# Later low halves, split sums of squares and a regrouped mixer projection in a two-block transformer kernel

## What is computed

```
def first_block(x, ...):                                  # DEPTH is 1
    x = x + 0.5 * rms_norm(swiglu(rms_norm(x, ffn1_pre_g[l]), ffn1_w_gu[l], ffn1_w_down[l]), ffn1_post_g[l])
    y = hybrid_mixer(rms_norm(x, mix_pre_g[l]), ...)      # RG-LRU and attention, then y @ w_o
    x = x + rms_norm(y, mix_post_g[l])
    x = x + 0.5 * rms_norm(swiglu(rms_norm(x, ffn2_pre_g[l]), ffn2_w_gu[l], ffn2_w_down[l]), ffn2_post_g[l])

def second_block(x, c, ctx, ...):                         # i = 0 a retention, i = 1 a neighbourhood attention
    for i in range(DEPTH_2):
        y_lat = mixer(modulate(h_lat, m_lat[0], m_lat[1]), ...)
        h_lat = layer_norm(DEEPNORM_ALPHA * h_lat + m_lat[2] * y_lat, ln_g[i, 0], ln_b[i, 0])
        f_lat = swiglu_2(modulate(h_lat, m_lat[3], m_lat[4]), ffn_w13[i], ffn_w2[i])
        h_lat = layer_norm(DEEPNORM_ALPHA * h_lat + m_lat[5] * f_lat, ln_g[i, 1], ln_b[i, 1])
        # in layer 0 the context h_ctx goes the same way

def swiglu(x, w_gu, w_down):
    gate, up = jnp.split(x @ w_gu, 2, axis=-1)
    return (jax.nn.silu(gate) * up) @ w_down
```

## Time and profile before

| | us |
|---|---|
| median of 3 runs (lowest and highest) | 3059.47 (3057.58 and 3062.56) |
| the profiled execution | 3062.67 |
| its span, first to last instruction | 3060.9 |
| PE busy | 2918.7 |
| DVE busy | 1477.6 |
| ACT busy | 1044.0 |
| POOL busy | 535.0 |
| mean granted TensorE clock, as a share of full speed | 0.977 |

### The profile page before, as it was taken

The page is one execution under the profiler, slowest core; times in us unless marked ns, Lnnn a source line. Parts: engine busy times, 40 slices in busy tenths (PEclk is TensorE's granted clock), DMA queues, the critical chain, the costliest instruction groups (busy, mean ns, idle before and its releaser), DMA issues.

```text
span 3060.9 us, 40191 instructions
## 1 busy us (share of the span) xinstructions
PE 2918.7 (95%) x16176; PEld 2480.4 (81%) x16176; DVE 1477.6 (48%) x2596; ACT 1044.0 (34%) x1813; POOL 535.0 (17%) x287
## 2 busy tenths in 40 slices
PE   7999989899998999999998899999998998999998
PEld 7888886888878868778685888888887777898887
DVE  5676569457674324242333735434564525642224
ACT  4322247442333422222222622122235535452222
POOL 1342200023231101111010011111102212012220
PEclk9999989899999999999999999999998999999999
DMA  3544312125443101111010023323312111122221
GB/s 137 177 158 169 107 64 74 65 90 173 149 160 123 58 28 62 49 48 63 28 62 21 29 90 119 102 74 109 128 49 89 56 57 66 63 76 105 102 95 37
DMA packets 84697, 268.81 MB, mean 88 GB/s; under 512 B 8992, under 2 KB 16544, under 8 KB 84128
## 3 DMA queue, kind: packets, MB, share of 16 engines
q1 hardware_dynamic: 84512, 266.25, 25.2%
HBM read 262.54 MB, written 2.10 MB: 86 GB/s over the span
## 4 chain that ended last, share of the span: by engine, by line
PE 61%; DVE 4%; ACT 2%; issue 1%; POOL 0%; DMA 0%; DVEq 0%; ACTq 0%; POOLq 0%; SPq 0%
PE ps L1348 18%; PE ps L1349 18%; PE ps L1350 18%; PE ps L1530 3%; PE ps L1580 1%; PE ps L1521 1%; PE ps L1564 1%; PE ps L1553 1%; ACT t_whi L1610 1%; DVE t_misc L1916 0%; ACT t_h L1659 0%; DVE t_x L1938 0%; DVE t_wlo L1896 0%; DVE t_tmp L2248 0%; DVE t_misc L2256 0%
## 5 line engine op out<-in xcount | busy, mean ns | idle before, releaser
L1348 PE MATMUL ps<-t_h,t_whi 128*128 128x512 f32 (+1 forms) x2368 | 830.2, 351 | 28.0 <-POOL t_wlo L2330 19.9
L1349 PE MATMUL ps<-t_h,t_wlo 128*128 128x512 f32 (+1 forms) x2368 | 825.5, 349 | 0.0
L1350 PE MATMUL ps<-t_h,t_whi 128*128 128x512 f32 (+1 forms) x2368 | 824.3, 348 | 0.0
L2330 POOL TENSOR_TENSOR t_wlo<-t_raw,t_whi 128x1024 fp32r<-128x1024 f32 (+3 forms) x147 | 356.6, 2426 | 1542.4 <-ACT t_whi L1610 1542.3
L1348 PEld LDWEIGHTS ps<-t_h,t_whi 128*128 128x128 f32 x2368 | 455.2, 192 | 90.5 <-issue 18.9
L1349 PEld LDWEIGHTS ps<-t_h,t_wlo 128*128 128x128 f32 x2368 | 455.5, 192 | 54.8
L1350 PEld LDWEIGHTS ps<-t_h,t_whi 128*128 128x128 f32 x2368 | 454.5, 192 | 55.4
L1348 PE MATMUL ps<-t_hid,t_whi 128*128 128x256 f32 (+1 forms) x1306 | 426.9, 327 | 11.2 <-DVE t_hid L2028 4.0
L1896 DVE TENSOR_TENSOR t_wlo<-t_raw,t_whi 128x1024 fp32r<-128x1024 f32 (+3 forms) x180 | 222.5, 1236 | 440.1 <-ACT t_whi L1610 439.9
L1610 ACT CAST t_whi<-t_raw 128x1024 fp32r<-128x1024 f32 (+3 forms) x327 | 326.3, 999 | 310.2 <-PE ps L1350 279.2
L1349 PE MATMUL ps<-t_hid,t_wlo 128*128 128x256 f32 (+1 forms) x1306 | 423.0, 324 | 0.0
(11 more groups left out here) (249 smaller groups left out, 3813.8 us busy)
## 6 DMA issues: line engine op xcount, KB each, us to landing
t_raw<-in_gu SPq DMA_DIRECT2D x176, 512.0 KB, 3.2
t_raw<-in_ada SPq DMA_DIRECT2D x96, 512.0 KB, 3.2
t_raw<-in_dn SPq DMA_DIRECT2D x52, 512.0 KB, 3.5
t_raw<-in_dn SPq DMA_DIRECT2D x24, 384.0 KB, 3.2
t_raw<-in_ret_v SPq DMA_DIRECT2D x16, 512.0 KB, 3.2
t_raw<-in_ret_qk SPq DMA_DIRECT2D x16, 512.0 KB, 3.2
t_raw<-in_ret_g SPq DMA_DIRECT2D x16, 512.0 KB, 3.1
t_raw<-in_ret_o SPq DMA_DIRECT2D x16, 512.0 KB, 3.5
```

The costliest lines, as they stand in the source:

```text
L1348: e.matmul(out, whi, xlo, start=first, stop=False, skip_group_check=shared)
L1349: e.matmul(out, wlo, xhi, start=False, stop=False, skip_group_check=shared)
L1350: return e.matmul(out, whi, xhi, start=False, stop=last, skip_group_check=shared)
L2330: e.tensor_tensor(m.block(1, it.slot, n), m.raw(it), m.block(0, it.slot, n), ALU.subtract).then_inc(*S["lo_pool"].of(j))
```

## The change

The number of products is the same; the order of items, the engine of some low halves and the grouping of one projection change.

- **Low halves.** `give` puts a block's `prep_lo` into a list `lows`. While a chain runs or blocks are held, one block stays in it, so a low half stands one block later than its high half; `ready(j)` writes it out ahead of the first product that needs it. The choice between VectorE and GpSimd keeps its rule, but falls otherwise in places, since two kinds of chain last longer.
- **Squares and sums.** The item `sum` was two instructions, one for ScalarE and one for VectorE, at one place. Now `square` is ScalarE's item, and `sum` stands one chunk later where chunks arrive one by one (`late`).
- **Root.** For s = 1 of a norm over squares the chain starts after 4.5 instead of 1.6 units, which puts `root_sum` and `root_row` two steps of TensorE later in nf1, nm and nf2 (and in mixp and f2p one or two steps later).
- **Late work.** The chains of `alpha` and `ln_out` start after 14.0 instead of 0.5 units. The last attention stage ends them before it moves x.
- **by_steps.** All drains of the four step groups stand ahead of the `over` calls, and so ahead of the next blocks' high and low halves.
- **Mixer.** `probs(0)` stands two steps earlier; one `release` stands earlier; the output projection starts with six blocks of the first 256 tokens and two of the next 256 in step groups, where it was seven and one, and the blocks that were held are prepared ahead of the drains.

```diff
@@ -157,6 +158,8 @@
         keys = [(which, i + k) for k in range(w)]
+        while any(k in it["keys"] for it in adds for k in keys):
+            put("sum", **adds.pop(0))
         return (0 if which == "a" else 1024) + i * 256, [e for k in keys for e in slots.get(k, [])], keys
...
@@ -197,24 +200,32 @@
         where[j] = slot
-        if chains or state["held"] is not None:
+        busy = chains or state["held"] is not None
+        if busy:
             low[j] = "lo_dve"
...
         put("prep", j=j, slot=slot, after=after, lo=low[j])
-        if state["held"] is None:
-            put("prep_lo", j=j)
-        else:
-            state["held"].append((None, j))
+        lows.append(j)
+        split(1 if busy else 0)
...
+    def split(keep=0):
...
+        while len(lows) > keep:
+            put("prep_lo", j=lows.pop(0))
...
+    def ready(j):
...
+        while j in lows:
+            split(len(lows) - 1)
+        return j
...
-        held = state["held"]
-        for i in [i for i, (slot, _) in enumerate(held) if slot is None][::-1]:
-            put("prep_lo", j=held.pop(i)[1])
-        if held:
-            give(*held.pop(0))
+        split()
+        if state["held"]:
+            give(*state["held"].pop(0))
...
@@ -277,12 +290,14 @@
                 yield
-            for g, j, post in zip(groups, held, posts):
-                if si == len(segs) - 1:
+            for g, post in zip(groups, posts):
+                post(g)
+            if si == len(segs) - 1:
+                for g, j in zip(groups, held):
                     over(j, "ps", g.id)
-                post(g)
             for (_, _, nk, src, outs), j in zip(specs[4:], held[4:]):
                 (_, emptier, post), = outs
+                ready(j)
                 b = following()
...
@@ -331,17 +346,25 @@
-    def sum_add(inst, s, c, tile, ready, square, after=()):
-        it = put("sum", inst=inst, s=s, c=c, tile=tile, ready=ready, square=square, after=list(after), off=0)
-        if square and c >= 2:
-            it["off"], it["after"], keys = tmp("a", 256)
-            free(keys, ("acc", (inst, s, c)))
+    def sum_add(inst, s, c, tile, ready, square, after=(), late=False):
+        it = dict(inst=inst, s=s, c=c, tile=tile, ready=ready, square=square, after=list(after), off=0, keys=[])
+        if square:
+            if c >= 2:
+                it["off"], it["after"], it["keys"] = tmp("a", 256)
+                free(it["keys"], ("acc", (inst, s, c)))
+            put("square", **it)
+            if c >= 2:
+                adds.append(it)
+                while len(adds) > (1 if late and c < DC - 1 else 0):
+                    put("sum", **adds.pop(0))
+        else:
+            put("sum", **it)
...
         first = 0 if square else 2
-        sum_add(inst, s, j, tile, ready, square, state["acc_free"] if first <= j < first + 2 else ())
+        sum_add(inst, s, j, tile, ready, square, state["acc_free"] if first <= j < first + 2 else (), True)
         if j == DC - 1:
-            chains[s] = [1.6, chain(s)]
+            chains[s] = [4.5 if square and s == 1 else 1.6, chain(s)]
...
@@ -381,7 +404,7 @@
         if c == DC - 1:
-            chains[s + 10] = [0.5, later("alpha", s=s)]
+            chains[s + 10] = [14.0, later("alpha", s=s)]
...
@@ -418,7 +441,7 @@
         if out:
-            chains[s + 10] = [0.5, later("ln_out", inst=inst, ln=ln, s=s)]
+            chains[s + 10] = [14.0, later("ln_out", inst=inst, ln=ln, s=s)]
...
@@ -630,14 +653,13 @@
                          seats=[0, 1, 2, 3, 4, 5, 7, 4, 6, 5])
-        between = {1: lambda: v_turn(0, 6), 4: lambda: scores(0), 7: lambda: scores(1)}
+        between = {1: lambda: v_turn(0, 6), 4: lambda: scores(0), 7: lambda: scores(1), 9: lambda: probs(0)}
         state["held"] = []
...
                 release()
-        probs(0)
         v_turn(1, 4)
...
@@ -698,12 +720,12 @@
         each("rec_e", (1,))
+        release()
         cols.append(root_sums("ya", 1, 1, heads, False))
...
         apply("ya", 0, 0, heads)
-        release()
         each("rec_g", (0, 1, 2))
...
@@ -727,8 +749,9 @@
         groups = []
-        for i, (j, t0) in enumerate([(j, 0) for j in range(7)] + [(0, 256)]):
+        for i, (j, t0) in enumerate([(j, 0) for j in range(6)] + [(0, 256), (1, 256)]):
             b = 4 + i // 2
+            ready(held[j])
             if i % 2 == 0:
...
@@ -741,44 +764,42 @@
-        o_step(4, groups[:7], 0)
-        o_step(5, groups[:7], 0)
+        o_step(4, groups[:6], 0)
+        o_step(5, groups[:6], 0)
         cols = [root_sums("yl", s, 2 + s, lru) for s in range(2)]
...
         apply("ya", 1, 1, heads)
-        o_step(6, groups[:7], 0)
+        o_step(6, groups[:6], 0)
         put("root_row", inst="yl", s=0, off=offs[0], bank=2)
         apply("yl", 0, 2, lru)
-        o_step(7, groups[:7], 0)
+        o_step(7, groups[:6], 0)
         put("root_row", inst="yl", s=1, off=offs[1], bank=3)
...
         for k in heads:
-            o_step(k, groups[7:], 256)
+            o_step(k, groups[6:], 256)
         for k in lru:
-            o_step(k, groups[:7], 0)
-            o_step(k, groups[7:], 256)
+            o_step(k, groups[:6], 0)
+            o_step(k, groups[6:], 256)
+        while state["held"]:
+            release()
         state["held"] = None
+        for g in groups[6:]:
+            over(g.w, "ps", groups[7].id)
         for g in groups:
             o_post(g.j)(g)
-        over(held[0], "ps", groups[7].id)
-        late = block(("w_o", 7), (SLOT,))
...
-        def o_rest(j, w, t0):
+        held.append(block(("w_o", 7), (SLOT,)))
+        for j, t0 in [(6, 0), (7, 0)] + [(j, 256) for j in range(2, 8)]:
             b = bank()
-            g = put("mm", w=w, slot=where[w], lo=low[w], base=0, nk=DC, src=("y",), t0=t0, n=256, bank=b, po=0,
+            ready(held[j])
+            g = put("mm", w=held[j], slot=where[held[j]], lo=low[held[j]], base=0, nk=DC, src=("y",), t0=t0, n=256, bank=b, po=0,
                     before=seat(b, "drain_act", len(items)))
...
             if t0:
-                over(w, "ps", g.id)
+                over(held[j], "ps", g.id)
             o_post(j)(g)
-            return ("ps", g.id)
...
-        o_rest(7, late, 0)
-        for j in range(1, 8):
-            last = o_rest(j, (held + [late])[j], 256)
-        state["hid_free"] = [last]
+        state["hid_free"] = [("ps", g.id)]
         state["misc_free"] = [("y_lo", (3, 1))]
...
@@ -926,6 +948,8 @@
             state["acc_free"] = [("drain_dve", ("na_s", 1, 15, hd)) for hd in range(2)] + [("bm", (1, 3, 2, 1)), ("d_misc", "mask2")]
+            for s in (10, 11, 12):
+                force(s)
             put("move_x")
```

12 lines of the change are left out of this document (7 added, 5 removed).

## The result

The changed kernel is slower. Its median is 3069.43 us (3065.61 to 3075.18, seven runs) against 3059.47 us (3055.47 to 3063.34, seven runs) of the kernel before: a ratio of 1.0035, interval 1.0021 to 1.0048. I had forecast 3037.7 us with 3022 to 3052 as the range. The sign is wrong, and the measured median lies 32 us above the forecast.

A forecast was written before the change was run, and what follows sets the result against it. TensorE, busy 95% of the span, was taken to bound the kernel, leaving its gaps and slow stretches to win. Gains of 28.3 us less losses of 6.5 gave net 21.8, from 3059.47 to 3037.7 us, range 3022 to 3052.

The forecast's parts named there:

- End of the first FFN: Stall of 8.52 us near 396 us: later root and lagging low halves leave two short waits; gain 8 us, bounds 3.5 and 12.5.
- the two new waits that I forecast: End of first FFN, 394 to 401 us: 1.2 us for block 71's low half, 1.4 us for mixp's `root_sum`.
- rival (b): Waits are passed on: a later `root_sum` only moves the wait to the diagonal or next sum; 11 us less, 3049 us; chance 0.22.
- the mixer's probabilities: At 453 us TensorE's wait of 2.04 us, with its clock, is covered by two earlier steps; gain 3.7 us.
- What gets worse: Four step groups in by_steps: drains ahead of the next low halves make new stalls; loss 6.5 us, bounds 2 and 16.
- Rival (c): Slower through drains ahead of low halves: long waits at all four step groups cost 48 us, kernel 3080 us; chance 0.04.
- Second and third norm: Near 603 us and the second FFN's end, later steps cover the sum waits; gains 2.9 and 7 us, diagonal's 3.05 us stays.
- Mixer's end: Stall near 565 us shrinks from 7.14 to 4.9 us with both casts ahead of the drains; gain 2.5 us, bounds 0 and 10.
- The start of its output projection: Mixer's output projection: four waits for low halves sum 6.1 us; gain 1 us, bounds -1 and 2.
- Late work: Later `alpha` and `ln_out`: gains 1 us at 849 and 1.1 us each at 2300 and 2668; 0 elsewhere.
- The clock: Half of each half-speed stretch behind a long stall counted as lost, busy part only; 1 us for the new stalls.

## Why the prediction was wrong

The sum had a net gain of 21.8 us, and the profiled execution has a loss of 10.5. By places (the table, and 960.9 us, where the changed kernel is 10.9 behind; gains are positive) the 32 us are: up to 376 us -5.1 for my -1.3; the end of the first FFN 8.5 for 8; 414 to 494 us -9.0 for 3.7; up to 558 -2.0 for 1; up to 606 4.8 for 5.4; up to 656 -6.1 for -1.7; up to 961 -2.0 for 1; up to 1041 2.8 for 7; the rest -2.4 for -0.3; and -1 of clock that I had at no place. The stretch from 414 to 494 us alone is 12.7 of the 32.

**End of the first FFN: right (8 us).** From 376.1 to 413.9 us the table has 8.5. But it isn't the squares and casts together that give it. The lag alone gives 5.6, the start alone 0.9, and undoing the sums in the changed kernel leaves 7.7 of 8.5. Of the two new waits that I forecast one came (1.90 us for 1.4); block 71's did not, and with the sums undone it is block 71's that comes (2.69 us at 401) and the other that does not. The waits for ScalarE that I counted on VectorE are eleven and not twelve (5.87 us), which changes nothing.

**Behind it: the step that failed.** I followed the later root to its own sum and diagonal and no further. I had written as rival (b) that a later root only moves the wait, priced 11 us in all, and gave it 0.22. Behind the root, the norm moved too: the stalls at 425.20 and 445.37 and their clock, from 414 to 494 us, cost 9.0 where my sum had a gain of 3.7 for the mixer's probabilities. The lag alone loses 2.5 us there and the start alone 3.0, and with either undone the changed kernel loses 2 to 3: it takes both. That 3.7 was itself wrong: the mixer part alone is 0.1 us ahead at 494 of where it was at 376. TensorE no longer waits for the probabilities at 453, but 3.21 us at 472.39 for ScalarE's copy of the turned probabilities out of PSUM.

**What gets worse: named, but priced at the wrong place.** I asked of each drain group only what stands behind it on VectorE. At 62.65 that is right (1.18 us for 1.3). What I left out is that the item moved, `over`, holds the load of a raw buffer as well. The price is paid 39 us later, through SP's queue, the conditioning and a drain (2.59 us and its clock at 101.57). Up to 100 us the changed kernel loses 5.1. At 650 I had 1.7 us for the drains, and the stretch from 606 to 656 costs 6.1 (2.3 with the order undone). From 1041 to 1800 us, which holds the third FFN's step groups, it cost 2.0 (8.1 to 10.1) where I had 2.5. Rival (c), slower through the drains ahead of the halves, named the part that in fact costs. Its own condition, 7 us a place, isn't met at any: some 2 to 5 us at three places were enough, since the gains beside them were smaller than I had them.

**Second and third norm (2.9 and 7).** From 580.5 to 605.6 us the changed kernel gains 1.9, and right behind comes the new sum at 636.21. At the third, the wait of 4.20 us went as I said, but the diagonal's behind it grew from 3.05 us to 4.90 and a half's of 1.71 follows. I had written that it stays. ScalarE explains it: the root's table load at 1005.81 stands behind ten steps of 0.58 us that make the next product's input. From 960.9 to 1041.0 us the gain is 2.8 of 7, where the lag alone gains 4.3.

**Mixer's end: right.** The stall is 4.62 us for my 4.9 and is ended by the copy. From 557.8 to 580.5 us 2.9 are gained for my 2.5; the mixer part alone has 3.3 there. **The start of its output projection** gains 2.5 with the mixer part alone (494 to 558), for my 1. In the changed kernel the profiled execution loses 2.0 there, as it ran 20.5 us at low clock behind a stall of 2.40 us. The kernel with the late work undone did the same (clock 0.50 in the same window). The one with the late work undone and even halves differs from it only from block 137 on, 300 us later, and yet had two stretches of 3.4 there. It gained 2.4 us from 494 to 558 where the other lost 1.8. The kernel with the sums undone had two stretches of 3.4 as well. The changed kernel's window:

```profile
535.04:555.50 20.46, 18.42 (x88) 18.12 (x87) 10.98 (x27) 7.52 (x15) 0.00 (x0) 0.51 0.17 52
```

Columns are window, its length, then busy us of TensorE, its weight load, VectorE, ScalarE and GpSimd, granted clock, DMA share and GB/s. So 4 to 5 us of a single trace at such a place are the clock's chance and not the change's.

**Late work:** 2668 came as forecast (1.49 for 2.61). Nothing was gained at 849 (2.79 for 2.52) or at 2300 (8.72 for 8.64), and the late work as a whole is 2.4 us to the bad if anything. What my sum put at nothing without a reason is what mixer and late work do to the deal between VectorE and GpSimd. Turned once from block 137 on, it is worth 17.6 us; turned by both it is back where it was, so it is no part of the 32 us, by luck. My section on the change named the late chains for it and missed the mixer part.

**The clock.** I took half of each low stretch behind a long stall and only 1 us for the new ones. The long stall's clock did come back (13.7 us of low clock at the first FFN's end are 6.8 now). But stalls of 1.65 to 2.8 us brought a stretch of 3.4 us each, at 425.20, 445.37 and 649.87 in the profiled execution, that is 1.7 us for each. All low stretches add up to 160.4 us where they were 143.8. Of these 16.6 us more, 10.3 lie near 535 us (20.5 for 10.2), so 5 of the 9.1 us of added busy time are that one chance and some 4 the rest. Without the long stretch, the profiled executions with the sums undone and with the late work undone and even halves are busy 2919.5 and 2918.4 us, as before, and have 2.9 and 4.1 us more of gaps. So how a loss divides into gaps and clock is not fixed from one execution to the next. The Trainium skill ("TensorE: Matmul & The Clock Gate", Part 1) counts the throttled time times the share withheld as the penalty. Here this gives 16.6 / 2 = 8.3 us of the difference, and the trace's rise in busy time (9.1) is near it. The part inside gaps that I had argued about (44 us of low clock before, 41 now) is a quarter to a third of the whole but almost cancels between the two kernels.

## What to carry over

When a step moves in a queue, follow every resource that it holds: here it also gives back a load buffer, and the price appeared 39 us later, in another stage, through a DMA queue that issues in order. Look at what the next stage has already queued before you start a chain's last step later. And where a kernel deals work to two engines in turn, look at who gets which item: the deal had been settled by accident, and turning it round was worth 17.6 us, against the 21.8 that the whole change was meant to bring. When parts of a change are run alone, hold such a deal fixed, and say so: the mixer part's own turn of it was hidden by the late work's.

## What the runs showed of the hardware

A wait of 1.65 us can cost as much again in clock as it lasts: behind 445.37 stood 3.4 us at half speed. It need not, since the same 1.65 us at 422.03 with the lag alone brought none. By these figures (an estimate) four waits of 2 us with 1.7 us of clock each would cost 14.8 us, where the one of 8.52 cost 12.0 with its clock. VectorE's scaling of 128x512 values (line 2281) took 0.49 us by itself (at 2381.48 in the kernel before), 1.06 beside GpSimd's small products (at 2380.32) and 1.62 beside GpSimd's low half, which ended at 2369.93 as that line ran. The Trainium skill ("Advanced Engine Details and Errata", VectorE Performance Modes) says that VectorE's second port to SBUF is shared with GpSimd and that the two block each other; these lengths agree. It is still the cheaper place for the half here: what slows is a step of 0.49 us, while on VectorE the half's whole 1.23 us stands ahead.
